# Copies and exponentials put in front of weight splits, two groups of the odd layer's attention begun among its projections, and another order of its loads

## The reference, cut to what matters

```python
def nsa_compress(t, pe, w1, w2):
    B, S, G, D = t.shape
    ch = t.reshape(B, S // CMP_STRIDE, CMP_STRIDE, G, D)
    blocks = jnp.concatenate([ch[:, :-1], ch[:, 1:]], axis=2)
    blocks = blocks + pe[:, None, :]
    flat = blocks.transpose(0, 1, 3, 2, 4).reshape(B, blocks.shape[1], G, CMP_LEN * D)
    return jax.nn.gelu(flat @ w1) @ w2
...
    s = jnp.where(dist >= 0, s, -jnp.inf)
    m = jnp.max(s, -1, keepdims=True)
    p = jnp.exp(s - m)
    den = jnp.sum(p, -1, keepdims=True)
```

## Time and profile before

| what | value |
|---|---|
| three timed runs | 1287.68, 1293.22, 1295.89 us, median 1293.22 |
| the profiled execution | 1291.83 us |
| its span | 1290.4 us |
| mean granted clock of TensorE | 0.981 |
| PE busy | 1240.0 us (96%) |
| DVE busy | 901.1 us (70%) |
| ACT busy | 608.4 us (47%) |
| cross-attention, 300 to 339 us | 4 groups |
| even layer, from projection 6 to attention's end | 598 to 690 us |
| odd layer, projections and attention | 923 to 1065 us |

### The profile page before, as it was taken

One profiled execution on the slowest core, in us unless ns is written; L12 is line 12 of the kernel. 1 busy time (PEld: TensorE's weight loads), 2 busy tenths in 40 slices (PEclk: granted clock), 3 DMA queues, 4 the chain that ended last, 5 costly groups with the idle time before them and its releaser, 6 DMA issues. The chain is left out here.

```text
span 1290.4 us, 21185 instructions
## 1 busy us (share of the span) xinstructions
PE 1240.0 (96%) x8525; PEld 1144.3 (89%) x8528; DVE 901.1 (70%) x1266; ACT 608.4 (47%) x917; POOL 107.8 (8%) x148
## 2 busy tenths in 40 slices
PE   8999999999999999999898999999998899999997
PEld 6888888988899999899888999999986899999996
DVE  5967995664667888845668757667655498666677
ACT  2352214453555666634554545654414364555452
POOL 3892000003000000010000000000200000000000
PEclk9999999989899999999999999999999699999999
DMA  9543444507535676624325356667356004555561
GB/s 281 180 141 115 130 147 163 192 28 230 170 117 174 219 229 211 213 68 158 105 72 190 131 185 210 218 225 167 99 159 199 14 1 164 167 192 193 176 211 42
DMA packets 178735, 202.76 MB, mean 157 GB/s; under 512 B 21885, under 2 KB 163164, under 8 KB 178637
## 3 DMA queue, kind: packets, MB, share of 16 engines
q1 hardware_dynamic: 175083, 191.49, 46.6%
q0 software_dynamic: 3184, 9.77, 2.4%
q10 hardware_dynamic: 369, 0.13, 0.1%
HBM read 200.30 MB, written 1.08 MB: 156 GB/s over the span
## 5 line engine op out<-in xcount | busy, mean ns | idle before, releaser
L1474 DVE TENSOR_TENSOR w_parts<-raw,w_parts 128x1024 fp32r<-128x1024 f32 (+1 forms) x242 | 294.9, 1218 | 143.2 <-ACT w_parts L1463 138.1
L1757 PEld LDWEIGHTS ps<-hT_parts,w_parts 128*128 128x128 f32 x2880 | 349.1, 192 | 1.9
L1757 PE MATMUL ps<-hT_parts,w_parts 128*128 128x256 f32 x2880 | 350.7, 283 | 0.0
L1463 ACT CAST w_parts<-raw 128x1024 fp32r<-128x1024 f32 (+1 forms) x242 | 252.9, 1045 | 184.8 <-PE ps L1757 70.3
L1776 PE MATMUL ps<-w_parts,gT_parts 128*128 128x512 f32 x720 | 169.5, 391 | 0.8 <-DVE w_parts L1474 0.8
L1776 PEld LDWEIGHTS ps<-w_parts,gT_parts 128*128 128x128 f32 x720 | 133.6, 188 | 28.1 <-DVE w_parts L1474 1.0
L1527 PE MATMUL ps<-hT_parts,w_parts 128*128 128x256 f32 x816 | 101.3, 285 | 2.0 <-DVE w_parts L1474 1.4
L1527 PEld LDWEIGHTS ps<-hT_parts,w_parts 128*128 128x128 f32 x816 | 99.0, 192 | 2.7 <-DVE w_parts L1474 1.7
L477 PE MATMUL ps<-hT,ring 128*128 128x256 f32 x448 | 100.1, 384 | 1.2 <-ACT hT L304 1.2
L477 PEld LDWEIGHTS ps<-hT,ring 128*128 128x128 f32 x448 | 85.6, 193 | 14.3 <-issue 1.6
L1881 DVE SCALAR_TENSOR_TENSOR arena_late<-ps,vecT,arena_late 128x255 f32<-128x255 f32 (+1 forms) x176 | 84.9, 482 | 11.0 <-ACT arena_late L1831 4.8
(11 more groups left out here) (414 smaller groups left out, 1587.5 us busy)
## 6 DMA issues: line engine op xcount, KB each, us to landing
raw<-in_ffn_w_up SPq DMA_DIRECT2D x44, 1024.0 KB, 5.1
raw<-in_f_w_up SPq DMA_DIRECT2D x22, 1024.0 KB, 5.3
raw<-in_ffn_w_down SPq DMA_DIRECT2D x22, 1024.0 KB, 5.0
ring<-in_w_in SPq DMA_DIRECT2D x18, 1024.0 KB, 5.8
raw<-in_ev_w_in SPq DMA_DIRECT2D x15, 1024.0 KB, 5.4
raw<-in_f_w_down SPq DMA_DIRECT2D x11, 1024.0 KB, 4.9
ring<-in_x_wkv SPq DMA_DIRECT2D x8, 1024.0 KB, 5.4
ring<-in_w_out SPq DMA_DIRECT2D x4, 1024.0 KB, 8.2
```

What stands on the lines that cost most here:

```text
L1463: self.done(A, A.copy(high[:, c], self.raw[:, u % RAW, c]), self.s_hi)
L1474: self.done(V, V.tensor_tensor(low[:, c], self.raw[:, u % RAW, c], high[:, c].bitcast(F32), ALU.subtract), self.s_lo)
L1757: mm = T.matmul(self.ps[:, b, m * 256:m * 256 + 256], w[:, kk, m * P:(m + 1) * P], x[:, kk, :], start=kk == 0 and q == 0, stop=kk == KD - ...
```

## The change

In cross-attention the split of the second `x_wo` unit moves behind ACT's copy 0 and exponential 1 and behind DVE's maximum 2. In the even layer the copies of transposes (`act_turned`, `dve_turned`) stand before the split of the same step, exponential 3 goes from step 10 to step 11 behind the copy out of that unit, exponential 4 before the copy out of unit 14, whose bank is 6 and not 5. In the odd layer the list of loads changes (key units earlier, `u_uv` before the third compress unit); the window branch comes before the compressed one in the first half of the tokens; groups 0 and 1 then read no compressed keys; scores 1, maximum 1 and exponential 1 are made before the loop; both compress products use bank 0 and the hidden parts bank 1; `XS` lies on `kfT`; the sigmoid of the gates is earlier; DVE's copies of the latent keys are spread.

```diff
         queries(1)
         compress(0)
+        keys(0)
         self.u_uq.append(unit(I["od_w_uq_2"][0], 512, 3, 256, False))
-        keys(0)
+        keys(1)
         compress(1)
-        keys(1)
         self.u_uk = unit(I["od_w_uk_2"][0], 0, 2, 512, False)
 
         self.u_odo = [unit(I["od_w_out_2"][0], 0)]
+        self.u_uv = unit(I["od_w_uv_2"][0], 0, 2, 512, False)
         compress(2)
-        self.u_uv = unit(I["od_w_uv_2"][0], 0, 2, 512, False)
         compress(3)
...
-    def act_attention(self, quarters, start=0, also={}):
+    def act_attention(self, quarters, start=0, also={}, made=1):
...
-            if i + 1 < n:
+            if start + made <= i + 1 < n:
                 self.act_exp(i + 1)
...
-        self.act_split(self.u_wo[WAY_OUT[1]])
-        self.act_attention({2: [0], 3: [2], 4: [1, 3]})
+        self.act_attention({2: [0], 3: [2], 4: [1, 3]}, also={0: lambda: self.act_split(self.u_wo[WAY_OUT[1]])})
...
-        self.dve_split(self.u_wo[WAY_OUT[1]])
-        self.dve_attention({2: [0], 3: [2], 4: [1, 3]})
+        self.dve_attention({2: [0], 3: [2], 4: [1, 3]}, also={0: lambda: self.dve_split(self.u_wo[WAY_OUT[1]])})
...
-        banks = {6: 6, 7: 7, 9: 5, 10: 7, 11: 7, 12: 6, 13: 4, 14: 5}
+        banks = {6: 6, 7: 7, 9: 5, 10: 7, 11: 7, 12: 6, 13: 4, 14: 6}
...
             elif c >= 6 and (c - 6) % 3:
+                if c == 14:
+                    self.act_exp(4)
                 self.act_evac(pf[c], B[(c - 6) // 3][(c - 6) % 3])
+            if 9 <= c <= 12:
+                self.act_turned(c - 9)
+            if c == 11:
+                self.act_exp(3)
             if c not in (*first, 14):
                 self.act_freed(self.u_ev[c])
             if c in (6, 7):
                 self.act_exp(c - 6)
-            if c in (9, 10):
-                self.act_turned(c - 9)
-                self.act_exp(c - 7)
-            if c in (11, 12):
-                self.act_turned(c - 9)
+            if c == 9:
+                self.act_exp(2)
...
+            if 9 <= c <= 12:
+                self.dve_turned(c - 9)
             if c not in (*first, 14):
                 self.dve_freed(self.u_ev[c])
...
+        XS = shaped(kfT.rearrange("p h n -> p (h n)")[:, 0:64 * NCMP], (2, 16, 2, NCMP))
...
+        uvf = self.pe_late(self.u_uv, "T", ckT)
         self.pe_compress(1, 0, XS)
-        uvf = self.pe_late(self.u_uv, "T", ckT)
+        self.pe_scores(1)
...
-        self.pe_scores(1)
         self.pe_attention({9: [(0, 2), (1, 3)], 10: [(2, 0)]})
...
         self.act_compressed(1, hidden)
-        self.done(A, A.activation(Gt[:, :, 0:24], Gt[:, :, 0:24], ACT.Sigmoid), self.s_gates)
+        self.act_exp(1)
...
-        self.act_attention({9: [0], 10: [1, 2]})
+        self.act_attention({9: [0], 10: [1, 2]}, made=2)
...
+        self.dve_max(1)
         self.dve_drain_plain(qtf, qfT)
         self.dve_hidden(0, hf_[0], hid)
-        self.dve_drain_plain(ktf, kfT)
+        self.dve_drain_plain(ktf[0:2], kfT, 4)
         self.dve_hidden(1, hf_[1], hid)
+        self.dve_drain_plain(ktf[2:3], kfT[:, 4:6, :], 2)
...
-        T, u, b = self.T, self.u_cmp[2 * kv + half], 2 * kv
+        T, u, b = self.T, self.u_cmp[2 * kv + half], 0
...
-        T, b = self.T, 3
+        T, b = self.T, 1
...
-            for br in (1, 0, 2) if t == 0 else (0, 1, 2):
+            for br in (1, 2, 0) if t == 0 else (0, 1, 2):
```

More of the change, by code:

```diff
@@ L1385, in late_units @@
         inner = [self.u_kv[0], self.u_kv[1], self.u_q[0], self.u_uq[0], self.u_q[1], self.u_cmp[0], self.u_uq[1], self.u_k[0],
-                 self.u_cmp[1], self.u_k[1], self.u_uk, self.u_cmp[2], self.u_uv, self.u_cmp[3]]
+                 self.u_cmp[1], self.u_k[1], self.u_uk, self.u_uv, self.u_cmp[2], self.u_cmp[3]]
         for out, ff, then in ((self.u_wo, self.u_ffn[0], [self.u_ev[c] for c in self.ev_order]),
@@ L2518, in even_layer @@
                 self.act_root(ss)
-        self.act_exp(4)
         A.wait_ge(*self.unit_done(self.u_ev[14]))
@@ L2555, in even_layer @@
             if c in (9, 10):
-                self.dve_turned(c - 9)
                 self.dve_max(c - 7)
-                if c == 10:
-                    self.dve_out(0)
-            if c in (11, 12):
-                self.dve_turned(c - 9)
+            if c in (10, 11, 12):
                 self.dve_out(c - 10)
@@ L2721, in odd_layer @@
         uq, qf, kf, vm = take(NT, 768), take(NT, 8, P), take(NT, 8, P), take(NT, 512)
-        KS, XS = self.place(0, 4, SEQ), self.place(1024, 2, 16, 2, NCMP)
+        KS = self.place(0, 4, SEQ)
         cqn, ckn, scr = self.place(1984, NT, 384), self.place(2752, NT, 256), self.place(3264, 384)
@@ L2801, in odd_layer @@
         self.act_split(self.u_k[1])
+        self.done(A, A.activation(Gt[:, :, 0:24], Gt[:, :, 0:24], ACT.Sigmoid), self.s_gates)
         self.act_compressed(0, hidden)
@@ L2853, in odd_layer @@
         self.drain(V, V.tensor_copy(vc[0:NCMP].rearrange("p a b -> p (a b)"), self.ps[0:NCMP, 1, 0:128]), vcf)
-        self.dve_max(1)
+        self.dve_drain_plain(ktf[3:4], kfT[:, 6:8, :], 2)
         self.dve_attention({9: [0], 10: [1, 2]})
@@ L2989, in out @@
             ins = V.tensor_tensor(yv, yv, self.tmp8[:, 0:nh, :], ALU.add)
-            if br == 2:
+            if br == (0 if t == 0 else 2):
                 self.done(V, ins, self.s_nsa)
```

## The result

The changed kernel took 1279.83 us (median of 6 executions, 1277.46 to 1281.66) where the kernel before, on the same chips, took 1294.11 (median of 6, 1287.68 to 1296.31). The ratio is 0.9897, with a 95% interval of 0.988 to 0.9915: about 1% faster, 14.3 us by the medians. I had forecast 1277.0 us and 16.1 us less.

What follows compares the result with a forecast made beforehand. TensorE, busy 96% of the span, was taken as the bound. Cross-attention -6.1, even layer -1.2 and odd layer -8.8 sum to -16.1 us, from the median 1293.2 to 1277 us; range for 8 in 10 runs 1270 to 1287.

Steps and rivals of the forecast that it cites:

- the likeliest case: Odd layer's attention: half clock to about 1010 us, then full; 1277 us in all, chance 0.44.
- Cross-attention: Wait of 3.80 us falls to 0.3 and the pieces behind it return to full clock: -6.1 us.
- the cross gain is eaten: Cross-attention: exponential 2 behind the split comes late; half the gain or less, 1282 us, chance 0.12.
- Even layer: Four waits of PE shrink or move: -1.2 us, bounds 0 and -6.2.
- The -0.3 of the wait: Even layer: values 2 start at 647.4 and not 647.68, only -0.3 of the 2.45 us wait.
- the -0.9 at the end: Even layer: the wait before 667.90 falls from 2.20 to 1.3 us, -0.9.
- Odd layer up to transposes 0: Scores 1 are done earlier, so transposes 0 start at 1002.9 and not 1006.01: -3.1 us.
- The key unit's 3.6 us: Odd layer: earlier key load removes 2.09 us idling and half clock; 3.6 us freed, but eaten by three things.
- Odd layer, attention: Transposes 0 to scores 5 end at 1022.1, not 1031.25; odd layer -8.8 us in all, bounds -1.6 and -13.4.
- The other side: Odd layer: new 1.9 us wait at 984.6 keeps the clock low until scores 5; 1295 to 1298 us, chance 0.05.
- Clock stays low: Odd layer: half clock from transposes 0 to scores 5, gain there only 1.6 us; 1284 us, chance 0.26.
- clock stays full: Odd layer: the 0.7 us wait at 1002 does not drop the clock, -13.4 us; 1272.5 us, chance 0.13.

Runs made afterwards that it cites:

- x_cross: The kernel before with the edit in cross-attention alone; 1287.86 us, ratio 0.9955.
- y_evfill: The changed kernel with eight matmuls of zeros in the even layer's 2.34 us wait of values 2; ratio 0.9907 to the kernel before.
- x_groups: The kernel before with only the new order of the odd layer's first three attention groups; ratio 1.0007.
- x_keys2: The kernel before with only the new order of the odd layer's first loads; ratio 0.9998.
- y_bank: The changed kernel with unit 12 of the even layer in bank 0 and not 6; 1277.77 us, ratio 0.988 to the kernel before.
- y_fill3: The changed kernel with matmuls of zeros in four TensorE waits of the odd layer; 1276.3 us, ratio 0.9865 to the kernel before.
- after2: The changed kernel run once more, as it is, beside the experiments; 1281.63 us, ratio 0.9915 to the kernel before.
- x_odd: The kernel before with the edits in the odd layer alone; 1288.72 us, ratio 0.9961.
- z_best: The changed kernel with even-layer unit 12 in bank 0, zeros in four odd-layer waits and three waits up to cross-attention; 1271.92 us, ratio 0.9845.

## Why the prediction was right, and where not

The forecast time (1277.0) lies 2.8 us under the measured one, which is inside the range, and the likeliest case was the one that came. The gain was forecast too large, though: 16.1 us are a ratio of 0.9876, just outside the interval of 0.988 to 0.9915. The stages of the two profiles give 12.6, all profiles some 12.5, and the medians 14.3 the first time and 10.6 the second. That the time fits within 3 us is in part the luck of the first measurement; about 3.5 us of gain were missing. The stages:

- **Cross-attention**, forecast -6.1, measured -6.42. Every step came as worked out: ACT's split starts at 323.28, which less 2.02 is 321.3; the wait is 0.22 and not 0.3; the full clock returns, worth nearly as much as the wait. Exponential 2 ends about 327.2, forecast 325.3 plus 2.0. The rival "the cross gain is eaten" is refuted by the stretch of x_cross. The size is that of one profile of before; against all six it is 4.2 to 7.1.
- **Even layer**, forecast -1.2, measured -0.16. The -0.3 of the wait that moves from values 1 to values 2 came (-0.24 up to values 2), and so did the -0.9 at the end. The step that failed is that I priced the moved wait at its length alone. I had written that a wait costs twice, and had an example for (2.09 us at 971) and one against (2.45 at 639.20); behind this one the clock fell, +1.6, and y_evfill shows that these are the clock's. Another -0.65 behind transposes 4, where the scores ran at full clock (1.46 us and not 2.62), I had left in the bounds. And the example against was no rule: behind the same wait of 2.45 us the clock fell in x_groups and x_keys2, so the old stage cost up to 1.2 us more than I had read.
- **Odd layer up to transposes 0**, forecast -3.1, measured 71.47 to 69.12, -2.35. The key unit's 3.6 us were won. The term that was mis-sized is the load of the compression weights: 1.49 and 2.36 us of waiting where I had 0.9 and 1.9. The bank's exponential ended at 981.9 and the matmuls began at 982.99, so the load decides, as I had it by the traced durations. By the fit from the Trainium skill, "DMA: Bandwidth & Descriptors", section "Anatomy of one DMA", the exponential would have decided. But the page gives that fit for DMAs that GpSimd issues, and SyncE issues these loads, so it was the wrong figure for them.
- **Odd layer, attention**, transposes 0 to maximum 5: forecast 1002.9 to 1022.1, that is 19.2 us, measured 999.12 to 1020.61, 21.49. Two sizes failed, both clock. Scores 3 were taken as half recovered, 2.4 us, and took 3.38. And I let transposes 3 and scores 5 run at full clock, 2.8 us, where they took 4.24 from start to DVE's maximum, since in a wait of 0.96 us that my timetable did not have the clock fell again. The order of events was as forecast: the 2.51 us wait is gone, DVE is the chain from maximum 5 on, with +0.2 where I had +0.4.
- **The other side**, the rival in which the 1.9 us wait lowers the clock and it stays low: refuted as a whole. The clock did fall behind that wait in y_bank and y_evfill, not in the changed kernel, and it cost 1.7 us (5.30 against 3.61) and not 10.
- "Clock stays low" and "clock stays full" were the right axis. (The pieces of the first add up to 25.4 us and not to about 26.) What I had not seen is that an edit can choose: with zeros in the waits the odd layer lost not 5.99 but 12.33 us (130.23 to 117.90), close to the 13.4 that I had set as the bound for no half clock at all.

The Trainium skill, "TensorE: Matmul & The Clock Gate", section "HAM oscillation", says that a wait for data between short bursts lets the clock fall and each burst starts slow. The rows here agree for the loop of the odd layer, and y_fill3 shows the reverse of it. But the waits of the page's example last about 3 to 5 us and bring the clock down every time. Here waits of 0.96 to 2.5 us did it as well, and the same wait did and did not.

## What to carry to other kernels

Where TensorE is the bound, price a wait in front of short matmuls at its length and, beside it, at the half clock of what follows; in this kernel the second part was 1.6 of 4.3 us in one place and most of 6.3 in another. Before moving work to remove such waits, try what matmuls of zeros into a free bank give: they need no new order, and they tell how much of a wait's cost is clock. And look at who holds a PSUM bank before blaming the engine that is named: one bank number was worth 4.3 us of its stretch, a third of what the whole change gave in the profiles.

## What the runs showed of the hardware that I had not expected

- Nearly the same wait at the same place does not always lower the clock. Ahead of the third compression PE idled 2.32 to 2.53 us in five profiles; behind it the 16 matmuls took 3.61 us in the changed kernel (2.36), after2 (2.33) and x_odd (2.53), and 5.30 in y_bank (2.35) and y_evfill (2.32). Ahead of transposes 0 it idled 1.17 us in the changed kernel, x_odd and y_bank, and the 128x7 products behind took 3.42, 1.85 and 3.42 us. The wait of 2.45 us ahead of values 1 in the old even layer lowered it in two of six profiles. The instructions ahead in the layer were the same; what decides between them was not measured. So a single profile gives a half clock's size only to within some 1.5 us.
- A short wait in a stretch of small matmuls can do it as well: the clock was 0.50 around the wait of 0.96 us at 1016 in the changed kernel. It need not fall behind the wait: in windows of half a microsecond it was 0.65 from 998.5 and 0.71 from 1015.5, both inside a wait and before PE began again, but at 643 it was still 1.00 when PE began and 0.66 half a microsecond later.
- Eight matmuls of zeros, 128x512 in bf16, took 1.89 us at full clock, and zeros kept it at 1.00 through waits that had brought it down; but not always, as the spell at 1004 us in z_best shows.
